# Two of the four gate logit products of a GLA head moved behind the first weight pair of its V chunk

## The reference

```python
def project(t):
    p = t @ w_in
    q, k, v, g = jnp.split(p, [GLA_KEY_DIM, 2 * GLA_KEY_DIM, 2 * GLA_KEY_DIM + GLA_VAL_DIM], axis=-1)
    ...
    las = [(jax.nn.log_sigmoid((tf @ gate_a1[d]) @ gate_a2[d] + gate_b[d]) / GLA_GATE_NORM
            ).reshape(bt, tt, GLA_HEADS, GLA_DK) for d in range(2)]
    return q, k, v, g, las[0], las[1]
```

## Time and profile before

| | |
|---|---|
| median of three runs | 1734.18 us |
| profiled execution | 1730.55 us |
| its span, first to last instruction | 1728.8 us |
| mean granted TensorE clock | 0.982 of full |
| PE busy | 96% of the span |
| DVE busy | 53% |
| ACT busy | 32% |

### The profile page before, as it was taken

How to read it: one execution, slowest core, us unless ns; L and a number is a source line. 1 busy time by engine, 2 the same in 40 slices (tenths; PEclk the granted TensorE clock), 3 DMA queues, 4 the chain that set the end, 5 groups by cost and what they waited for, 6 DMA issues and landing times.

```text
span 1728.8 us, 19289 instructions
## 1 busy us (share of the span) xinstructions
PE 1657.5 (96%) x7870; PEld 1262.0 (73%) x7870; DVE 908.0 (53%) x1528; ACT 546.2 (32%) x792; POOL 2.2 (0%) x9
## 2 busy tenths in 40 slices
PE   4889999999999999989999799999999999999998
PEld 3457877787778777857777587887787778777777
DVE  4327442644265445445333457475665657475864
ACT  3214332333144333332222324232323233232532
POOL 0000000000000000000000000000000000000000
PEclk9799999999999999989999899999999999999999
DMA  8994344532542245215455326343523533442444
GB/s 312 382 368 155 123 135 159 193 117 70 182 171 86 63 169 183 86 61 173 161 202 181 135 77 234 98 134 122 183 89 118 177 130 120 132 136 86 149 155 135
DMA packets 155421, 265.55 MB, mean 154 GB/s; under 512 B 10458, under 2 KB 94356, under 8 KB 146596
## 3 DMA queue, kind: packets, MB, share of 16 engines
q1 hardware_dynamic: 149856, 256.28, 43.9%
q10 hardware_dynamic: 5476, 8.03, 1.4%
HBM read 262.18 MB, written 2.10 MB: 153 GB/s over the span
## 4 chain that ended last, share of the span: by engine, by line
PE 90%; DVE 5%; DMA 2%; ACT 2%; issue 1%; SPq 0%; ACTq 0%; DVEq 0%
PE bank L858 69%; PE bank L1187 4%; PE bank L816 3%; PE bank L1047 2%; PE bank L994 2%; PE bank L1115 2%; PE bank L1131 2%; PE bank L790 1%; DVE w_lo L1214 1%; DMA u<-in_ctx 1%; DVE work L1299 1%; ACT w_hi L499 1%; DMA u<-in_ada_w 1%; DVE work L1541 1%; PE bank L990 1%
## 5 line engine op out<-in xcount | busy, mean ns | idle before, releaser
L1214 DVE TENSOR_TENSOR w_lo<-w_raw,w_hi 128x1024 fp32r<-128x1024 f32 x288 | 350.5, 1222 | 528.8 <-ACT w_hi L499 528.7
L858 PE MATMUL bank<-w_lo,acts_hi 128*128 128x512 f32 x1536 | 617.6, 402 | 11.1 <-DVE acts_lo L1322 5.7
L858 PE MATMUL bank<-w_hi,acts_hi 128*128 128x512 f32 x1536 | 600.5, 391 | 0.0
L858 PE MATMUL bank<-w_hi,acts_lo 128*128 128x512 f32 x1536 | 600.3, 391 | 0.0
L499 ACT ACTIVATE w_hi<-w_raw 128x1024 fp32r<-128x1024 f32 x288 | 302.9, 1057 | 879.1 <-PE bank L858 803.3
L858 PEld LDWEIGHTS bank<-w_lo,acts_hi 128*128 128x128 f32 x1536 | 289.5, 189 | 106.8 <-issue 30.6
L858 PEld LDWEIGHTS bank<-w_hi,acts_lo 128*128 128x128 f32 x1536 | 289.5, 188 | 62.1
L858 PEld LDWEIGHTS bank<-w_hi,acts_hi 128*128 128x128 f32 x1536 | 290.0, 189 | 60.0 <-issue 3.1
L858 PE MATMUL bank<-acts_hi,w_lo 128*128 128x512 f32 x256 | 104.8, 409 | 7.0 <-DVE acts_lo L1344 7.0
L858 PE MATMUL bank<-acts_hi,w_hi 128*128 128x512 f32 x256 | 101.6, 397 | 0.0
L858 PE MATMUL bank<-acts_lo,w_hi 128*128 128x512 f32 x256 | 101.4, 396 | 0.0
(11 more groups left out here) (183 smaller groups left out, 1273.0 us busy)
## 6 DMA issues: line engine op xcount, KB each, us to landing
ada_w<-in_ada_w SPq DMA_DIRECT2D x64, 1024.0 KB, 7.8
w_raw<-in_diff_w_in SPq DMA_DIRECT2D x256, 256.0 KB, 3.0
w_raw<-in_gla_w_in SPq DMA_DIRECT2D x64, 512.0 KB, 3.7
w_raw<-in_gla_w_in SPq DMA_DIRECT2D x64, 256.0 KB, 3.0
u<-in_ada_w SPq DMA_DIRECT2D x32, 512.0 KB, 9.7
w_raw<-in_gla_w_out SPq DMA_DIRECT2D x32, 512.0 KB, 3.9
w_raw<-in_diff_w_out SPq DMA_DIRECT2D x32, 512.0 KB, 4.3
ada_w<-in_ada_w SPq DMA_DIRECT2D x28, 512.0 KB, 9.7
```

The source lines that it names most:

```text
L858: last = pe.matmul(bank[t][:], a, b, start=(k == 0 and i == 0), stop=(k == NK - 1 and i == 2))
L1214: dve.tensor_tensor(w_lo[:, p % RING], raw[:, p % RING], w_hi[:, p % RING].bitcast(F32), ALU.subtract)\
```

## The change

`gate_logits` takes a list of products. Products 0 and 2 stay in front of the V chunk. Products 1 and 3 are issued by the `after` hook of the V chunk's pair 0, ahead of the two background quads that stand there. Nothing else is touched: DVE, ACT and SP have the same instructions in the same order.

```diff
-            def gate_logits(h):
+            def gate_logits(h, ns):

                 pe.wait_ge(a2_in, h * 64 + 64)
-                for n in (0, 2, 1, 3):
+                for n in ns:
                     rows = slice(2 * G_RANK, 4 * G_RANK) if n < 2 else slice(0, 2 * G_RANK)
                     if n == 3:
                         pe.wait_ge(logit_out, h * 4 + 1)
...
-                gate_logits(h)
-                project(c + 1, lambda t: c + 1, True,
-                        after=lambda p: unit_scores(h, 0) if p == 5 else None)
+                gate_logits(h, (0, 2))
+
+                def between(p):
+                    if p == 0:
+                        gate_logits(h, (1, 3))
+                    elif p == 5:
+                        unit_scores(h, 0)
+
+                project(c + 1, lambda t: c + 1, True, after=between)
```

## The result

The changed kernel takes 1747.37 us (median of four runs, 1743.81 to 1749.01) against 1733.49 us for the kernel before (median of four, 1731.3 to 1737.45): 13.9 us more, ratio 1.0079 with a 95% interval of 1.0055 to 1.0103. The profiled execution is the fastest of the four, 1743.81 us with a span of 1742.0 us, 13.2 us above the span before.

A forecast was written before the change was run, and what follows sets the result against it. PE, busy for 96% of the span, was taken to bound the kernel. Late quads net of the seam's gain, +8.2 us, plus the clock, +2.8, gave +11.0 on the median of 1734.2: 1745 us, range 1732 to 1751.

The forecast's parts named there:

- The seam and the moved products: PE ahead of and behind pair 0: seam of 3.1 us shrinks to 1.1, moved products cost 1.1; gain 0.95 a head.
- VectorE's block: DVE's unbroken run of subtract, scan and `low` behind the bias adds: starts 6.0 us later, since product 1's add comes later.
- The consumers: Three that wait for DVE's late run: pair 3's `low` and `unit_scores` at no cost, pair 4's `low` delaying SP's loads.
- SP's queue and the quads: Loads behind pair 4's `low` land late for PE behind pair 3: +3.4, +4.0, +1.8, head 0 -0.95, sum +8.2 us.
- The clock: PE's clock drops after the stops for the quads: two of three heads, +2.8 us, bounds 0 to +4.3.
- PE's waits: PE waits for the DMA of ada_w in heads 1 to 3, 4 to 5 us a head in two pieces.
- Rival 1: Quads behind pair 3 stay hidden, only the seam's gain is left: -3.8 us, 1730 us; chance 0.09.
- Rival 3: PE's stall at the quads is there but smaller: +3 to +5 us, 1737 to 1739 us; chance 0.08.
- Rival 2: Quads hidden, but the clock falls behind pair 0 in all four heads: +2 us, 1736 us; chance 0.05.

The follow-up runs named there:

- a_021: Changed kernel with products 0, 2 and 1 in front and only product 3 behind pair 0; 1739.82 us, ratio 1.0059 to the kernel before.
- a_early: Changed kernel with the two quads behind pair 3 issued early by SP (p = 2, not 4) in heads 1 to 3; 1726.65 us, ratio 0.9974.
- a_fill: Changed kernel with pair 4's split after the first product and the `low` of pairs 3 and 4 in VectorE's gap between adds; 1726.84 us, ratio 0.9971.
- a_take4: Changed kernel, SP's order untouched, but PE takes the quads behind pair 4 instead of pair 3 in heads 1 to 3; 1726.32 us, ratio 0.9970.
- a_pair1: Changed kernel with products 1 and 3 behind pair 1 instead of pair 0, and the quads issued early at p = 2; 1733.2 us, ratio 1.0016.
- b_late: Kernel before, all four products in front, with the quads behind pair 3 issued late, at p = 6, in heads 1 to 3; 1760.25 us, ratio 1.0164.
- b_early: Kernel before, four products in front, with the quads behind pair 3 issued early, at p = 2, in heads 1 to 3; 1730.32 us, ratio 0.9998.
- b_p13: Kernel before with the quads behind pair 3 issued one position later, at p = 5, in heads 1 to 3; 1734.0 us, ratio 1.0012.
- a_head2: The change made in head 2 alone, the other heads as in the kernel before; 1737.62 us, ratio 1.0045.

## Why the prediction was right

**The seam and the moved products.** Predicted: 1.1 us each, a gain of 0.95 us a head. Measured: 1.06 and 1.11 us, and head 0, which has nothing else, gains 0.94 us. The price of products between pairs and quads, for which no row stood, was the one chosen.

**VectorE's block.** Predicted 6.0 us later; measured 9.8 - 3.9 = 5.9 us. The `low` of pair 4 starts 21.0 us behind the first product, where 21.1 were forecast. a_021 shows that the in-order wait for the last add sets it.

**The consumers.** Pair 3's `low` and `unit_scores` were priced at nothing, and a_early, a_fill and a_take4, all with a late block, show no wait of PE's matmuls for them. a_pair1 finds the end of the room at pair 3's `low` first, as the list of consumers had it.

**SP's queue and the quads.** This was the step that decided, and three separate cures (issue early, `low` out of the block, take them later) and one separate cause (b_late) confirm it. Forecast ends of the quads: +3.4, +4.0, +1.8 and -0.95 us, together 8.2; measured +4.0, +4.4, +2.3 and -0.9, together 9.7.

One reading in this step was wrong. The times to landing of the earlier trace rows count from the start of an issue and not from its end. The chain shows it: in head 2 of the changed kernel SP's second issue starts at 502.27, and the transfer is counted from there, 8.18 us.

```profile
502.27 0.42 SPq L352 DMA_DIRECT2D ada_w<-in_ada_w  x1
```

So before the change the quads of head 2 landed at 498.3 and 500.8, and the room was 4.0 and 2.4 us, not 3.7 and 2.0. All three heads were forecast 0.4 us too late. With the right reading the sum is +3.6, +2.9, +1.4 and -0.95, together 6.9 us, and the second quads landed within 0.3 us of where it has them.

**The clock.** Predicted +2.8 us, with drops in two of three heads, 1.4 us each, on the pairs behind. Measured: drops in all three, +1.6, +0.8 and +0.5 us on the pairs behind, 2.9 in all. Four of the six quads ran at the lower clock as well. Each head's second quad took 1.0 us longer, 3.0 us in all, and nothing in the prediction stood for that. The clock cost 5.9 us in place of 2.8. That the total came out near the forecast is in part luck: the landings were taken 0.4 us too late in three heads, 1.3 us together, and the clock was taken 3.1 us too low.

The sentence drawn from the Trainium skill (TensorE: Matmul & The Clock Gate, "HAM oscillation"), a drop in all three heads, came nearer than my two. The waits in the page's example are longer, 3 to 5 us; the stops here were 0.6 to 2.8 us.

**PE's waits.** Forecast: 4 to 5 us a head in two pieces. Measured: 3.9, 3.4 and 3.8 us. In head 2, where 3.5 and 1.5 were worked out, they are 2.75 and 0.61: the quads landed 0.7 to 0.9 us sooner than forecast, 0.4 of it by the wrong reading, and the first quad itself ran slowly, 1.94 us, and filled 1.0 us of what would have been the second stop.

The profiled execution was forecast at 1741.5 us and took 1743.8; the median was forecast at 1745 and is 1747.4. The other three executions of the changed kernel are 3 to 5 us above the profiled one, with a mean granted clock of 0.977 against 0.979. That more of the clock's drops make this difference is argued, not shown: those executions have no trace here.

Rival 1 fell by the waits in the trace. Rival 3, a smaller stall, fell as well: the stall was larger than the forecast. Rival 2 fell too: in a_early products and quads stand side by side, 2.9 us in which the array is partly used, and the granted clock is 1.00 in the windows of 4 us that hold them and in those behind, in head 3 as shown and in the other heads.

## What to carry to other kernels

When an instruction moves, list what stands behind its consumer on the consumer's engine, and then what stands behind each of those on theirs. Here the way from two small products to a lost 4 us a head led over VectorE (its adds, and behind them a `low`), SP's order of loads and the DMA, and PE's own line showed only the gain. An in-order engine's idle gap is the place for work that another queue waits for: moving two `low` into VectorE's gap turned +0.8% into -0.3%. And read the room of every prefetch next to a place of change as landing time against time of use; it was 2.4 us in head 2, against a delay of 6. Check first from which end of the issue a landing is counted.

## What the runs showed of the hardware

- Two products on different groups of 32 partitions take 1.06 to 1.13 us together, one alone 1.05 to 1.12 us (seams, and a_021 behind pair 0); products 0, 2 and 1 in a row take 1.91 us (a_021).
- PE's clock after stops for a transfer: stops of 2.42 + 1.44, 2.75 + 0.61 and 2.30 + 1.45 us with one quad between were followed by the lower level each time, and after the stop of 2.75 us the first quad already ran at it. 1.22 + 1.45 and 1.00 + 1.42 us gave no drop, 1.50 + 1.42 us did; four single stops of 1.6 us between full pairs (a_pair1) gave none. With first stops 1.2 to 1.3 us shorter, a_021 is 2.9 and 1.9 us faster than the changed kernel in heads 1 and 3, from the first product to the end of the two pairs behind the quads, and 0.7 us slower in head 2, where the clock fell again.
- Pair 0 of head 3 takes 7.22 to 7.29 us in all five traces that have the four products in front of it (the kernel before, b_early, b_late, b_p13, a_head2), and 5.66 to 5.67 us in the six where the seam has no wait for VectorE, a_021 with its three products in front among them. In heads 0 to 2 no trace has a slow pair 0, with the wait or without. Why head 3 alone has it is open.
- The second of the two 1 MB loads, from the start of its own issue, landed after 7.8 to 9.05 us in heads 1 to 3 where SP issued it at p = 4 or later, and after 6.5 to 6.6 us at p = 2 in a_early and b_early. In a_pair1, also at p = 2, it was 8.5 us in head 1 and 6.7 in head 2. At the same place in the program it differed by up to 1.2 us between traces (head 3: 7.8 before, 9.05 in b_p13 one position on; head 2: 8.2 in the changed kernel, 9.0 in a_head2). What sets it is not shown; a room of 1 us can't be relied on.
